# Bias and query rows spread by DMA, and a token-major end of the last layer, in a two-layer hybrid decoder kernel

## The reference, cut to what matters

```python
h = rmsnorm(x, norms[0]) * (1 + sc1) + sh1
aq, ak, av, af, bq, bk, bv, bg, ca, cb = split_cols(h @ w_in)
logf = log_sigmoid(af + b_f)
# forgetting attention, 4 heads of 128
logits = q @ k.T * scale + cum[:, :, :, None] - cum[:, :, None, :]   # cum: running sum of logf over the keys
o_a = softmax(where(kpos <= qpos, logits, -inf)) @ v
# the 8 samples attend to 256 cached keys each, by the same formula, one query row per sample
o_b = retention(...)   # chunks of 128
o_c = conv module(...)
x = x + g1 * rmsnorm(concat([o_a, o_b, o_c]) @ w_o, norms[1])
h2 = rmsnorm(x, norms[2]) * (1 + sc2) + sh2
a, b = split(causal_dwconv(h2 @ ffn_up), 2)
x = x + g2 * rmsnorm((silu(a) * b) @ ffn_down, norms[3])
```

## Time and profile before

| | us |
|---|---|
| median of 3 runs | 2929.05 |
| lowest, highest of the runs | 2920.84, 2933.04 |
| the profiled execution, its time | 2917.62 |
| its span, first to last instruction | 2915.4 |
| TensorE busy in it | 2777.1 |
| VectorE busy | 1762.6 |
| ScalarE busy | 1189.8 |
| GpSimd busy | 201.3 |
| mean granted TensorE clock, of full speed | 0.972 |

### The profile page before, as it was taken

How to read it: one execution, slowest core, us unless ns; L and a number is a source line. 1 busy time by engine, 2 the same in 40 slices (tenths; PEclk the granted TensorE clock), 3 DMA queues, 4 the chain that set the end, 5 groups by cost and what they waited for, 6 DMA issues and landing times. The chain is left out here.

```text
span 2915.4 us, 46421 instructions
## 1 busy us (share of the span) xinstructions
PE 2777.1 (95%) x18668; PEld 2449.4 (84%) x18668; DVE 1762.6 (60%) x2839; ACT 1189.8 (41%) x1897; POOL 201.3 (7%) x102
## 2 busy tenths in 40 slices
PE   5999999999999999999759999999999999999996
PEld 3888888788788899999738888897877888999995
DVE  4594444546776766676645743444567667667665
ACT  2241333634444444444332323345444445444442
POOL 1211001120000000000021210012000000000000
PEclk7999999999999999999869999999999999999998
DMA  6752112353333333323158311234432333333321
GB/s 220 226 141 51 53 45 64 90 166 94 94 94 94 91 91 95 94 88 95 33 193 239 93 44 51 52 88 117 133 99 87 98 90 98 91 93 90 95 87 69
DMA packets 430644, 293.57 MB, mean 101 GB/s; under 512 B 26493, under 2 KB 392613, under 8 KB 429630
## 3 DMA queue, kind: packets, MB, share of 16 engines
q1 hardware_dynamic: 426128, 288.45, 33.5%
q10 hardware_dynamic: 4302, 2.15, 0.3%
HBM read 267.68 MB, written 23.71 MB: 100 GB/s over the span
## 5 line engine op out<-in xcount | busy, mean ns | idle before, releaser
L1731 PE MATMUL tslot<-g_hi,w_hi 128*128 128x260 f32 (+1 forms) x2496 | 670.5, 323 | 9.5 <-DVE g_lo L2313 6.1
L1731 PE MATMUL tslot<-g_hi,w_lo 128*128 128x260 f32 (+1 forms) x2496 | 664.9, 321 | 0.0
L1731 PE MATMUL tslot<-g_lo,w_hi 128*128 128x260 f32 (+1 forms) x2496 | 662.5, 320 | 0.0
L1731 PEld LDWEIGHTS tslot<-g_hi,w_hi 128*128 128x128 f32 x2496 | 413.9, 188 | 52.1 <-issue 6.9
L1731 PEld LDWEIGHTS tslot<-g_hi,w_lo 128*128 128x128 f32 x2496 | 413.2, 188 | 37.8
L1731 PEld LDWEIGHTS tslot<-g_lo,w_hi 128*128 128x128 f32 x2496 | 413.4, 188 | 37.3
L1702 ACT ACTIVATE w_hi<-w_raw 128x1024 fp32r<-128x1024 f32 x292 | 307.1, 1052 | 334.3 <-PE tslot L2090 311.8
L1706 DVE TENSOR_TENSOR w_lo<-w_raw,w_hi 128x1024 fp32r<-128x1024 f32 x276 | 336.0, 1218 | 1.5 <-ACT w_hi L1702 1.5
L2398 DVE TENSOR_TENSOR cat<-cat,tslot 128x512 f32<-128x512 f32 (+1 forms) x320 | 220.3, 690 | 192.5 <-PE tslot L2090 191.2
L2090 PE MATMUL tslot<-f_hi,w_hi 128*128 128x260 f32 (+1 forms) x1056 | 283.2, 323 | 6.1 <-DVE w_lo L1706 3.9
L2090 PE MATMUL tslot<-f_hi,w_lo 128*128 128x260 f32 (+1 forms) x1056 | 281.8, 322 | 0.0
(11 more groups left out here) (335 smaller groups left out, 3839.8 us busy)
## 6 DMA issues: line engine op xcount, KB each, us to landing
w_raw<-in_ffn_up_dram SPq DMA_DIRECT2D x176, 512.0 KB, 3.9
w_raw<-in_ffn_down_dram SPq DMA_DIRECT2D x88, 512.0 KB, 3.8
x_res<-in_ada_w_dram SPq DMA_DIRECT2D x64, 512.0 KB, 5.8
w_raw<-in_w_in_dram SPq DMA_DIRECT2D x46, 512.0 KB, 4.8
a_raw<-in_ada_w_dram SPq DMA_DIRECT2D x8, 2048.0 KB, 21.1
w_raw<-in_w_o_dram SPq DMA_DIRECT2D x32, 512.0 KB, 5.7
x_hold<-x_res SPq DMA_DIRECT2D x2, 4128.0 KB, 15.6
x_res<-x_hold SPq DMA_DIRECT2D x2, 4128.0 KB, 12.7
```

The lines of the kernel that those rows point to most:

```text
L1731: last = pe.matmul(out[:, at + a:at + b], w[:, kk, :], x[:, kk, t0 + a:t0 + b], start=(kk == 0 and first), stop=(kk == KD - 1 and w is w_lo))
```

## The change

1. Bias: the running sums are written head by head, TensorE turns them once per layer into 32 rows of 128 (`turn_bias`, pass 1), VectorE copies them to SBUF, and a DMA on ScalarE's queue stores them in DRAM (`hold_bias`). For each head one DMA loads the row of 1024 to all 128 partitions (`load_bias`). The diagonal, the spread and the copy go.
2. Queries: the new queries of a head go to DRAM (`hold_query`) and one DMA loads all 8 x 128 of them to every partition (`load_query`), feature by feature with the samples innermost, into the buffer of the retention's `kz` and `vt`. `multiply` reads them from there in two products.
3. Last layer: rows of `x` for both halves are turned in the hf 1 loop, four groups of two at the up tiles 1 to 4 (tokens 512 on, before the feed-forward's addition) and four at 16 to 19 (tokens 0 to 511, final) and copied out by ScalarE right behind the gate; the first half's `y` is stored from there. The end of hf 1 is token-major: squares and gated copies on ScalarE, turns on TensorE, and the inverse applied per partition, on VectorE for five of the eight blocks and on ScalarE and GpSimd for three. `block_exit` goes.
4. The memset of the inverse stands ahead of its wait.

```diff
-        SPREADS = {14: (0, 0), 20: (0, 1), 23: (1, 0), 29: (1, 1), 32: (2, 0), 33: (2, 1), 37: (3, 0), 38: (3, 1)}
+        bias_rows = sq[0][0:HA * NC8, 0:P]
+        Q_LOADS = {12: 0, 21: 1, 30: 2, 34: 3}
+        PRODUCTS = {14: (0, 0), 20: (0, 1), 23: (1, 0), 29: (1, 1), 32: (2, 0), 33: (2, 1), 37: (3, 0), 38: (3, 1)}
...
+            def turn_bias():
+                pe.wait_ge(cum_read, 1)
+                pe.matmul(x_bank[0:HA * NC8, P:2 * P], k.ncum[:, :], ident, start=True, stop=True).then_inc(bias_turned, 1)
...
-                if i == 0:
-                    pe.wait_ge(bias_moved, h + 1)
+                if i == 0 and h == 0:
+                    pe.wait_ge(att_done, NC8)
+                elif i == 0:
+                    pe.wait_ge(top, NC8 * h)
...
-                pe.wait_ge(prod_done, 2 * HA)
+                pe.wait_ge(g_scaled, 12)
...
+                if p == 1:
+                    turn_bias()
...
-                    act.wait_ge(bias_ready, h + 1)
-                    act.activation(bias, sc[:, :], ACT.Copy).then_inc(bias_moved, 1)
...
+                    if at == 7 and h < HA - 1:
+                        load_bias(h + 1)
...
+            def hold_bias():
+                act.wait_ge(bias_moved, 1)
+                act.dma_start(k.bias_hold[L].rearrange("h (c n) -> (h c) n", n=P), bias_rows).then_inc(bias_held, 16)
+
+            def load_bias(h):
+                if h == 0:
+                    act.wait_ge(bias_held, 16)
+                else:
+                    act.wait_ge(top, NC8 * h)
+                act.dma_start(bias, k.bias_hold[L, h:h + 1].to_broadcast([P, TP])).then_inc(bias_loaded, 16)
+
+            def hold_query(h):
+                act.wait_ge(new_done, 3 * h + 2)
+                act.dma_start(k.q_hold[L, h], k.q_new[:, h, :]).then_inc(q_held, 16)
+
+            def load_query(h):
+                act.wait_ge(q_held, 16 * (h + 1))
+                if h == 0:
+                    act.wait_ge(up_ready, NC8)
+                else:
+                    act.wait_ge(prod_done, 2 * h)
+                act.dma_start(q_all[:, :], k.q_hold[L, h:h + 1].rearrange("o n s -> o (n s)").to_broadcast([P, S * DA])).then_inc(q_loaded, 16)
...
+                if p == 2:
+                    hold_bias()
+                if p == 4:
+                    load_bias(0)
+                if p % 9 == 6 and p // 9 < HA:
+                    hold_query(p // 9)
+                if p in Q_LOADS:
+                    load_query(Q_LOADS[p])
...
-                dve.tensor_scalar(k.ncum[:, :], x_bank[:, 0:NC8 * HA], -1.0 / A_SCALE, None, ALU.mult).then_inc(cum_read, 1)
+                dve.tensor_scalar(k.ncum[:, :].rearrange("p (h c) -> p h c", h=HA),
+                                  x_bank[:, 0:NC8 * HA].rearrange("p (c h) -> p h c", h=HA), -1.0 / A_SCALE, None,
+                                  ALU.mult).then_inc(cum_read, 1)
...
+            def move_bias():
+                dve.wait_ge(bias_turned, 1)
+                dve.tensor_copy(bias_rows, x_bank[0:HA * NC8, P:2 * P]).then_inc(bias_moved, 1)
...
-                    dve.wait_ge(bias_moved, h + 1)
+                    dve.wait_ge(bias_loaded, 16 * (h + 1))
...
-                dve.wait_ge(q_spread, 2 * h + half + 1)
-                dve.tensor_tensor(prod, pages[h][:, :, 512 * half:512 * half + 512], bc((x_bank if h >= 2 else o_bank)[:, :], 1, NPG),
-                                  ALU.mult).then_inc(prod_done, 1)
+                dve.wait_ge(q_loaded, 16 * (h + 1))
+                q_half = q_all[:, :].rearrange("p (n s) -> p s n", s=S)[:, 4 * half:4 * half + 4, :]
+                for pg in range(NPG):
+                    op = dve.tensor_tensor(prod[:, pg, :].rearrange("p (s n) -> p s n", n=DA),
+                                           pages[h][:, pg, 512 * half:512 * half + 512].rearrange("p (s n) -> p s n", n=DA), q_half, ALU.mult)
+                    op.then_inc(k.quiet if pg == 0 else prod_done, 1)
...
+    def dve_inverse(self, dve, which, read=None):
+
+        n, link = self.n, self.lk
+        link(dve.memset(self.v[:, 0:n], 1.0))
         dve.wait_ge(self.sums_ready, which + 1)
-        link(dve.memset(self.v[:, 0:n], 1.0))
+        if read is not None:
+            dve.sem_inc(read, 1)
...
+        x_row = lambda c, half: k.rows_lo[:, 2 * c + half, 0:512]
+        y_row = lambda c, half: k.rows_hi[:, 2 * c + half, 0:512]
+        y_gated = lambda kk: k.rows_hi[:, kk, 512:1024]
+        s_row = lambda half: k.rows_lo[0:S, half, 512:1024]
+        y_bank = [[slot[1][:, 0:BANK], slot[1][:, BANK:2 * BANK], misc[0][:, :], misc[1][:, :]],
+                  [slot[0][:, 0:BANK], slot[0][:, BANK:2 * BANK], slot[2][:, BANK:2 * BANK], slot[2][:, 0:BANK]]]
+        FINAL_POOL = ((0, 3), (1, 1), (1, 3))
...
+            if final:
+                sp.wait_ge(y_moved, 2 * 4)
+                for c in range(4):
+                    sp.dma_start(d["y_prompt"][0, P * c:P * c + P, :].rearrange("p (h n) -> p h n", h=2),
+                                 k.rows_hi[:, 2 * c:2 * c + 2, 0:512]).then_inc(y_stored, 16)
...
+            if final:
+                done = [0, 0]
+                for half in range(2):
+                    for c in range(4):
+                        by_pool = (half, c) in FINAL_POOL
+                        done[by_pool] += 1
+                        sp.wait_ge(pool_rows if by_pool else row_done, done[by_pool])
+                        sp.dma_start(d["y_prompt"][0, 512 + P * c:512 + P * c + P, 512 * half:512 * half + 512],
+                                     x_row(c, half)).then_inc(stored, 16)
+                sp.wait_ge(row_done, 8 - len(FINAL_POOL) + 2)
+                sp.dma_start(d["y_sample"][:, 0, :].rearrange("p (h n) -> p h n", h=2),
+                             k.rows_lo[0:S, 0:2, 512:1024]).then_inc(stored, 16)
+            if final:
+                sp.wait_ge(y_stored, 16 * 4)
+            sp.wait_ge(stored, 16 * (11 + 9 * final))
...
+                    if final and j == PAIRS - 1 and c == 1:
+                        turn_samples()
+                    if final and j == PAIRS - 1 and c == 6:
+                        turn_gated(0)
...
+            def turn_rows(signal, moved, n, first):
+                c, half = divmod(n, 2)
+                if n >= 2:
+                    pe.wait_ge(moved, n - 1)
+                for j in range(4):
+                    at = P * (first + c)
+                    last = pe.transpose(misc[half][:, P * j:P * j + P], k.x[:, 4 * half + j, at:at + P], ident)
+                last.then_inc(signal, 1)
+
+            def turn_samples():
+                pe.wait_ge(tail_moved, 2)
+                for half in range(2):
+                    for j in range(4):
+                        last = pe.matmul(misc[half][0:S, P * j:P * j + P], k.x[:, 4 * half + j, TP:NT], ident, start=True, stop=True)
+                last.then_inc(s_turned, 1)
+
+            def turn_gated(half):
+                if half == 0:
+                    pe.wait_ge(s_moved, 2)
+                    pe.wait_ge(up_moved, 4 * PAIRS)
+                else:
+                    pe.wait_ge(gathered, KD * PAIRS)
+                for c in range(4):
+                    if (half, c) == (1, 3):
+                        pe.wait_ge(inv_read, 1)
+                    for j in range(4):
+                        kk = 4 * half + j
+                        if c == 0:
+                            pe.wait_ge(gated, kk + 1)
+                        last = pe.transpose(y_bank[half][c][:, P * j:P * j + P], y_gated(kk)[:, P * c:P * c + P], ident)
+                    last.then_inc(yt_turned, 1)
+
+            def turn_gated_samples():
+                pe.wait_ge(row_done, 2)
+                for half in range(2):
+                    for j in range(4):
+                        last = pe.matmul(y_bank[0][half][0:S, P * j:P * j + P], k.cat[:, 4 * half + j, TP:NT], ident, start=True, stop=True)
+                last.then_inc(yt_turned, 1)
...
+                    if final and hf and half == 0 and kk == 6 and 1 <= i <= 4:
+                        for n in (2 * i - 2, 2 * i - 1):
+                            turn_rows(x_turned, x_moved, n, 4)
+                    if final and hf and half == 0 and kk == 6 and 16 <= i <= 19:
+                        if i == 16:
+                            pe.wait_ge(ends[0].dve_added, KD)
+                        for n in (2 * i - 32, 2 * i - 31):
...
+            if final:
+                turn_gated(1)
+                turn_gated_samples()
+            else:
+                ends[1].pe_rb(pe, 0)
...
+            if final:
+                for n, (half, c) in enumerate(FINAL_POOL):
+                    pool.wait_ge(scaled_out, n + 1)
+                    pool.tensor_tensor(x_row(c, half), x_row(c, half), y_row(c, half), ALU.add).then_inc(pool_rows, 1)
...
+            def move_rows(turned_, moved_, row, c):
+                for half in range(2):
+                    act.wait_ge(turned_, 2 * c + half + 1)
```

(48 more changed lines are left out.)

136 lines of the change are left out of this document (39 added, 97 removed).

## The result

Before: 2929.28 us, median of 4 runs (2920.84 to 2933.04). After: 2899.47 us, median of 4 (2894.37 to 2900.88). The ratio is 0.9909, with a 95% interval of 0.9887 to 0.9932: 27 us by the ratio, 30 by the medians. The profiled executions are 17.0 apart (span 2915.4 and 2898.4). The forecast was 41 on the median. So the time fell inside the range, and the gain was a quarter to a third smaller than the sum said.

What follows compares the result with a forecast made beforehand. TensorE, busy 95% of the span, was taken as the bound, with a chain of waits at the end. Terms -27.4 + 0.4 + 6.4 - 20.4 = -41.0 took 2929.05 to 2888, range 2873 to 2903.

Steps and rivals of the forecast that it cites:

- the sum: Whole kernel: mixer, feed-forward loop and end together give -41.0 us, from 2929.05 to 2888.
- Mixer, out: TensorE in the mixers: 8 bias spreads (14.4) and 16 query spreads (13.0) go, 27.4; bias-row turns add 0.4.
- The multiply: VectorE's query product in the mixer, now two halves at a step of 8 elements: no penalty, 0 on the path.
- The upper bound of 5: Most the multiply could cost if the step doubled its time: 6 times about 0.9, some 5 us.
- Rival B: VectorE's chain bounds passes 20, 29 and 38: 1.9 at six places, 11 us, giving 2899; chance 0.11.
- the forecast's slack of 0.36: Pass 38: VectorE's normalize, without its wait for the spread, ends at 530.56, leaving 0.36 before TensorE turns the rows.
- Rival A: Mixer's broadcast loads land late, VectorE and TensorE wait; decides from 20 us per load, 2944 at 22; chance 0.03.
- Hooks: Feed-forward loop: sixteen groups of four added turns, two groups in each of eight tiles, cost TensorE 6.4 us.
- rival C: Hooks wait for ScalarE at each tile, 1.4 eight times, eating 11 of the end's 14: 2899; chance 0.12.
- The end: Last stretch of the kernel: end moves from 2915.4 to 2895.05 by a shorter chain, gain 20.4 us.
- The close point at ScalarE: At the end, ScalarE's square and gated copy take 1.46 per tile against TensorE's 1.43; no wait taken, bound 2 us.

Runs made afterwards that it cites:

- before_pad: The kernel before with one of its two bias spread products made twice for head 0 of each layer; median 2937.09 against 2923.14, ratio 1.0046.
- query_rows: The kernel after with held query rows written sample by sample and multiplied at unit step in one product of 1024; median 2897.71, ratio 0.9911.
- bias_only: The kernel before with only the bias rows by DMA, query rows still spread by TensorE and multiplied out of PSUM; median 2914.13, ratio 0.9967.

## Why the prediction came near, and what failed in it

- **Mixer, out, 27.4 less 0.4.** The counting held. Measured with the multiply at unit step it is 26.0: 6.6 per layer for the bias (7.0 forecast; half a spread costs 0.86 to 0.88 in before_pad, so a spread 1.7 and not 1.8) and 6.4 for the query (6.5).
- **The multiply, "I see no penalty for the step and take 0 for the path": the step that failed.** It costs 2 x (13.0 - 10.85) = 4.3, of which TensorE stands still for 3.6, at passes 29 and 38 of each layer (pass 20 had slack). 0.209 for 32 elements is nearly all fixed cost, so it could show nothing of a cost per element; I let it decide. The upper bound of 5 was right.
 The Trainium skill (SBUF — State Buffer, section "Door 1: The DMA port swizzle") says that each access to a new line of 16 bytes costs extra, which spoke against the step of 32 bytes. The runs agree with it: 1.1 to 1.2 for 512 elements, against 1.22 for 1024 at unit step in query_rows.
- **Rival B** was half right: TensorE waits at four places, by 0.7 and 1.1, not by 1.9 at six. In pass 29 it is the step alone, with 1.03 more of VectorE and the forecast's slack of 0.36. In pass 38 it is step and GpSimd, but the slack there was larger than the 0.36 read from it: VectorE takes 2.26 longer (3.48 for 1.22) and TensorE waits 1.13.
- **Rival A**: loads of 3.6 and 3.9 against the 20 at which it decides. False.
- **Hooks 6.4**: 7.1 (7.0 in the other traces that have them), or 0.88 for eight turns instead of 0.80. TensorE waited at none, so rival C's first half is false.
- **The end -20.4**: -16.9. Of the 3.5 missing, 1.2 come in ahead of the inverse: at full clock the sample turns take 1.85 (2868.93 to 2870.78) and the turns of the four gated tiles 1.67 (2878.07 to 2879.74), where 1.6 each were forecast, and half clock lasts 5.2 into the tile where it lasted 4.0 before, which is 0.6 more not granted. 1.5 is the wait for the turns of the samples' gated columns. The sum has no term for these: it lays the turns of the second half "beside the rsqrt chain and the first rows", and the samples' sixteen need banks that come free only with the first two rows. 0.8 lies between the last rows and the end; its cause stays open. The close point at ScalarE cost nothing.
- **The sum.** Measured by TensorE's starts it is -21.7 + 7.1 - 16.9 = -31.5, not -41, and 5.0 of it is clock at the end. By runs it is 27 to 30: what the end gives back of the clock, the starts of the blocks take again, since a mixer 10.85 shorter starts the next block at another place, and in all four block starts traced of this kernel at a worse one. No term of my sum had that, and the profile before could hardly show it. The 11 us by which the profiled execution lay under its median are in part such a difference: by the clock in its result it had 81.6 not granted, as few as the least of the 53 executions (mean 90.6), and 9 fewer at 0.80 is 7 us. The three runs of that median have no clock on record.

## What to carry to other kernels

Cost an operand's step from a row long enough that the elements weigh; a short operation shows only its fixed cost. The product that gave up its PSUM operand for one in SBUF was now also held off by GpSimd, so count both on the engine's slack in the pass where it is tight. And where TensorE is the bound, separate its work from its clock: compare starts of the same instructions, list the granted clock of untouched stretches, and try the kernel before with a microsecond added ahead, before a few missing us are put down to an edit.

## What the runs showed of the hardware that I had not expected

- 0.9 us more TensorE work in each mixer cost 14 us of 2923: in its trace the start of the next block had 8.5 and 6.8 us more not granted, in the same code. In 14 traces the length of such a start, 143.7 to 150.0, follows from where it falls against the moments at which the clock changes.
- A multiply of two SBUF operands runs to 2.0 to 2.5 beside a GpSimd subtraction, at either step; with one operand in PSUM it was never above 1.223 (bias_only), not even where it began inside a subtraction (before, pass 38: 527.85, with GpSimd from 526.31 to 528.68).
- Written as 1024 pieces of 4 bytes (query_rows), the last head's query rows let their load be issued only 10.9 later and held ScalarE for 5; the query load itself stayed at 3.9, and the bias loads landed in 7.9 in the median, against 3.6. None of it reached TensorE.
